# Per-layer embedding of a two-layer streaming encoder: projection before the gates, gates folded into h one by one

## What is computed

```python
for i in range(DEPTH):                       # DEPTH = 2
    h = h + 0.5 * swiglu(rms_norm(h, norm_ff1[i]), w1_ff1[i], w3_ff1[i], w2_ff1[i])
    z = rms_norm(h, norm_mix[i]) @ w_in[i]
    mix = concat([fox_attention(..), s5_mixer(..), retention(..), swa_sink_attention(..)])   # from z
    h = h + mix @ w_out[i]
    h = h + 0.5 * swiglu(rms_norm(h, norm_ff2[i]), w1_ff2[i], w3_ff2[i], w2_ff2[i])
    # per-layer embedding: p is (DEPTH, BATCH, 512, 256), w_ple_proj 256x1024, w_ple_gate 1024x1024
    h = h + (p[i] @ w_ple_proj[i]) * sigmoid(rms_norm(h, norm_ple[i]) @ w_ple_gate[i])
```

## Time and profile before

| | |
|---|---|
| runs (us) | 2390.26, 2395.86, 2398.57; median 2395.86 |
| profiled execution, span from first to last instruction | 2392.5 us |
| PE busy | 2273.6 us (95%) |
| PEld, DVE, ACT, POOL busy | 71%, 40%, 32%, 37% |
| mean granted TensorE clock | 0.954 of full speed |
| HBM traffic | 189.09 MB read, 2.10 MB written, 80 GB/s |

### The profile page before, as it was taken

The page is one execution under the profiler, slowest core; times in us unless marked ns, Lnnn a source line. Parts: engine busy times, 40 slices in busy tenths (PEclk is TensorE's granted clock), DMA queues, the critical chain, the costliest instruction groups (busy, mean ns, idle before and its releaser), DMA issues.

```text
span 2392.5 us, 26535 instructions
## 1 busy us (share of the span) xinstructions
PE 2273.6 (95%) x9180; PEld 1692.2 (71%) x9180; DVE 962.3 (40%) x1296; ACT 769.3 (32%) x1080; POOL 891.0 (37%) x388
## 2 busy tenths in 40 slices
PE   7999999878899999999989999997798999999999
PEld 5888887444457888888868888874454578888887
DVE  5222224868355422222362222248673553222124
ACT  4333223211253333322343332232113443333222
POOL 3444444433102444444344444444331034444442
PEclk9999999888789999999999999998897899999999
DMA  4222333111101222233222223331111022222332
GB/s 137 97 96 96 95 91 122 47 35 44 51 1 53 97 96 96 94 97 99 80 80 98 95 97 96 96 117 45 44 36 50 1 72 95 96 96 93 97 95 84
DMA packets 56087, 192.13 MB, mean 80 GB/s; under 512 B 6216, under 2 KB 6344, under 8 KB 55760
## 3 DMA queue, kind: packets, MB, share of 16 engines
q1 hardware_dynamic: 51840, 180.38, 23.4%
q10 hardware_dynamic: 4176, 10.84, 1.4%
HBM read 189.09 MB, written 2.10 MB: 80 GB/s over the span
## 4 chain that ended last, share of the span: by engine, by line
PE 42%; issue 37%; POOL 15%; DVE 4%; ACT 1%; POOLq 1%; DMA 0%; DVEq 0%; ACTq 0%; SPq 0%
PE psum L658 36%; POOL w_lo L591 14%; PE psum L814 2%; PE psum L717 1%; DVE s5b L1342 1%; PE psum L715 1%; POOL s5sin L611 1%; POOL s5cos L611 1%; DVE s5cos L1344 1%; DVE s5a L1340 0%; PE psum L728 0%; PE psum L905 0%; POOLq L590 0%; DVE s5sin L1345 0%; PE psum L744 0%
## 5 line engine op out<-in xcount | busy, mean ns | idle before, releaser
L591 POOL TENSOR_TENSOR w_lo<-w_raw,w_hi 128x1024 fp32r<-128x1024 f32 (+2 forms) x352 | 831.6, 2364 | 1469.2 <-ACT w_hi L954 1469.1
L658 PE MATMUL psum<-xh,w_hi 128*128 128x512 f32 x1856 | 734.6, 396 | 25.0 <-DVE xl L1178 25.0
L658 PE MATMUL psum<-xl,w_hi 128*128 128x512 f32 x1856 | 725.5, 391 | 0.0
L658 PE MATMUL psum<-xh,w_lo 128*128 128x512 f32 x1856 | 725.4, 391 | 0.0
L954 ACT ACTIVATE w_hi<-w_raw 128x1024 fp32r<-128x1024 f32 (+2 forms) x352 | 359.9, 1022 | 729.1 <-PE psum L658 706.2
L658 PEld LDWEIGHTS psum<-xh,w_hi 128*128 128x128 f32 x1856 | 350.0, 189 | 126.8 <-DVE xl L1178 28.9
L658 PEld LDWEIGHTS psum<-xl,w_hi 128*128 128x128 f32 x1856 | 350.3, 189 | 74.7 <-issue 2.9
L658 PEld LDWEIGHTS psum<-xh,w_lo 128*128 128x128 f32 x1856 | 350.1, 189 | 73.6
L658 PE MATMUL psum<-gh,w_lo 128*128 128x512 f32 x704 | 278.1, 395 | 0.0
L658 PE MATMUL psum<-gh,w_hi 128*128 128x512 f32 x704 | 278.1, 395 | 0.0
L658 PE MATMUL psum<-gl,w_hi 128*128 128x512 f32 x704 | 278.1, 395 | 0.0
(11 more groups left out here) (218 smaller groups left out, 1842.5 us busy)
## 6 DMA issues: line engine op xcount, KB each, us to landing
w_raw<-in_w SPq DMA_DIRECT2D x208, 512.0 KB, 3.3
w_raw<-in_w SPq DMA_DIRECT2D x64, 448.0 KB, 3.3
w_raw<-in_w_in SPq DMA_DIRECT2D x40, 512.0 KB, 3.3
w_raw<-in_w_out SPq DMA_DIRECT2D x16, 512.0 KB, 3.3
w_raw<-in_w_gate SPq DMA_DIRECT2D x16, 512.0 KB, 3.2
h<-in_x_t ACTq DMA_DIRECT2D x8, 256.0 KB, 8.0
dec<-in_decay ACTq DMA_DIRECT2D x2, 1024.0 KB, 5.2
w_raw<-in_w_proj SPq DMA_DIRECT2D x8, 256.0 KB, 2.6
```

The lines of the kernel that those rows point to most:

```text
L591: nc.gpsimd.tensor_tensor(lo[:, 0:tiles, :], raw[:, 0:tiles, :], hi[:, 0:tiles, :].bitcast(F32), ALU.subtract).then_inc(*w_ready.inc(times))
L658: mm = nc.tensor.matmul(out_ap, w[:, t, :], x[:, k0 + t, :], start=(first and t == picks[0] and n == 0), stop=(last and t == picks[-1] and ...
```

## The change

The projection units come first in the per-layer embedding, ahead of the gate units, in the loads, the splits and on PE. ACT copies the projection tiles out of PSUM into SBUF (`proj`, in the feed-forward's buffer, which is free by then); they rotate over banks 0, 1 and 2. `ph` and `pl`, the two parts of p, move to the small work area and are made right behind the last gate tile of the feed-forward's first half. Then the norm's matmul and the gate units follow. DVE takes each gate through to `h` at once: times `rstd`, wait for ACT's sigmoid (in place, in `t_sig`), times `proj`, added to `h`. PE signals in the last gate unit after each tile that this tile of `xh`/`xl` has been read (`x_free`), and ACT waits for this before it writes `xh` of the next layer. The number of matmuls, activations for gates, weight bytes and units is as before; 8 activations (copies) per layer are new.

```diff
@@ tables and banks
+U_PROJ = 4
-    return 4 if u >= BASE["ple"] + KD else 8
+    return 4 if BASE["ple"] <= u < BASE["ple"] + U_PROJ else 8
     b.claim(("norm", "ple"), 3)
     for dt in range(KD):
+        b.claim(("proj", dt), dt % 3, closes=(dt % 2 == 0))
         b.claim(("gate", dt), 4 + dt % 2, closes=False)
-        b.claim(("proj", dt), 6 + dt % 2, closes=(dt % 2 == 0))
+        ph = place("ph", [P, 2, T], m_off, F32R)
+        pl = place("pl", [P, 2, T], m_off + 2 * ROW, F32R)
+        t_sig = place("t_sig", [P, 2, T], m_off + 8 * ROW)
-        ph = place("ph", [P, 2, T], g_off, F32R)
-        pl = place("pl", [P, 2, T], g_off + 2 * ROW, F32R)
-        gate = place("gate", [P, KD, T], g_off + 4 * ROW)
+        proj = place("proj", [P, KD, T], g_off)
...
@@ PE
+                    if free and t != picks[-1]:
+                        mm.then_inc(*free.inc())
...
                 ff(L, 1)
-                for dt in range(KD):
-                    ps = open_bank(L, ("gate", dt))
-                    unit(L, BASE["ple"] + dt, dt, ps[:], xh, xl, 0, KD, True, True, x_done(L, 3) if dt == 0 else None)
-                    if dt == 0:
-                        norm(L, "ple", 3)
                 pe.wait_ge(*p_ready.at(L, 1))
-                for q in range(4):
-                    pe.wait_ge(*w_ready.at(L, BASE["ple"] + KD + q + 1))
+                for q in range(U_PROJ):
+                    pe.wait_ge(*w_ready.at(L, BASE["ple"] + q + 1))
...
+                norm(L, "ple", 3)
+                for dt in range(KD):
+                    ps = open_bank(L, ("gate", dt))
+                    unit(L, BASE["ple"] + U_PROJ + dt, dt, ps[:], xh, xl, 0, KD, True, True,
+                         x_done(L, 3) if dt == 0 else None, free=x_free if dt == KD - 1 else None)
@@ ACT
                 act.wait_ge(*h_ready.at(L, KD * (n - 1) + k + 1))
+                if n == 0 and k < KD - 1:
+                    act.wait_ge(*x_free.at(L, k + 2 - KD))
+                elif n == 0:
+                    act.wait_ge(*unit_done.at(L, 0))
                 nc.scalar.activation(xh[:, k, :], h[:, k, :], ACT.Copy, scale=gain[:, k:k + 1])\
...
                 feed_forward(L, 1)
+                act.wait_ge(*silu_ready.at(L, 2 * NF))
+                act.wait_ge(*p_in.at(L, 1))
+                nc.scalar.activation(ph[:], p_raw[:], ACT.Copy).then_inc(*ph_ready.inc())
                 for k in range(KD):
                     for u in range(3):
                         high(L, BASE["ffb1"] + 3 * k + u + SLOTS)
                     prepare(L, 3, k, par[:, PAR["g_ple"]])
-                act.wait_ge(*p_in.at(L, 1))
-                act.wait_ge(*unit_done.at(L, BASE["ple"]))
-                nc.scalar.activation(ph[:], p_raw[:], ACT.Copy).then_inc(*ph_ready.inc())
+                for k in range(KD):
+                    if k % 2:
+                        act.wait_ge(*unit_done.at(L, BASE["ple"] + k // 2 + 1))
+                        ps = psum[banks.bank[("proj", k)]]
+                    else:
+                        ps = full(L, ("proj", k))
+                    nc.scalar.activation(proj[:, k, :], ps[:], ACT.Copy).then_inc(*proj_ready.inc())
+                    if k % 2:
+                        high(L, BASE["ple"] + k // 2 + SLOTS)
                 root(L, "ple")
                 for k in range(KD):
                     act.wait_ge(*tg_ready.at(L, k + 1))
-                    nc.scalar.activation(gate[:, k, :], t_gate[:, k % 2, :], ACT.Sigmoid).then_inc(*sg_ready.inc())
-                    high(L, BASE["ple"] + k + SLOTS)
+                    nc.scalar.activation(t_sig[:, k % 2, :], t_sig[:, k % 2, :], ACT.Sigmoid).then_inc(*sg_ready.inc())
+                    if k < KD - SLOTS:
+                        high(L, BASE["ple"] + U_PROJ + k + SLOTS)
@@ DVE
-                add_and_prepare(L, 2, "ffb1", par[:, PAR["g_ple"]], 3, 0.5)
+                dve.wait_ge(*gl_ready.at(L, 2 * NF))
                 dve.wait_ge(*ph_ready.at(L, 1))
                 V.tensor_tensor(pl[:], p_raw[:], ph[:].bitcast(F32), ALU.subtract).then_inc(*p_ready.inc())
+                add_and_prepare(L, 2, "ffb1", par[:, PAR["g_ple"]], 3, 0.5)
                 invert(L, 4)
                 for k in range(KD):
-                    dve.wait_ge(*unit_done.at(L, BASE["ple"] + k + 1))
-                    if k >= 2:
-                        dve.wait_ge(*sg_ready.at(L, k - 1))
-                    V.tensor_tensor(t_gate[:, k % 2, :], psum[4 + k % 2][:], rstd[:], ALU.mult)\
-                        .then_inc(*tg_ready.inc())
-                for k in range(KD):
+                    dve.wait_ge(*unit_done.at(L, BASE["ple"] + U_PROJ + k + 1))
+                    t = t_sig[:, k % 2, :]
+                    V.tensor_tensor(t, psum[4 + k % 2][:], rstd[:], ALU.mult).then_inc(*tg_ready.inc())
                     dve.wait_ge(*sg_ready.at(L, k + 1))
...
-                    V.tensor_tensor(t_up[:, k % 2, :], ps[:], gate[:, k, :], ALU.mult).then_inc(*pm_ready.inc())
+                    dve.wait_ge(*proj_ready.at(L, k + 1))
+                    V.tensor_tensor(t, t, proj[:, k, :], ALU.mult).then_inc(*pm_ready.inc())
                     dve.wait_ge(*pm_ready.at(L, k + 1))
-                    V.tensor_tensor(h[:, k, :], h[:, k, :], t_up[:, k % 2, :], ALU.add).then_inc(*h_ready.inc())
+                    V.tensor_tensor(h[:, k, :], h[:, k, :], t, ALU.add).then_inc(*h_ready.inc())
```

More of the change, by code:

```diff
@@ L499, in trunk_kernel @@
         sg_ready = signal("sg_ready", KD)
+        proj_ready = signal("proj_ready", KD)
+        x_free = signal("x_free", KD - 1, before=KD - 1)
         dve_step = signal("dve_step", DVE_STEPS)
@@ L527, in trunk_kernel @@
             reader[("gate", i)] = (tg_ready, i + 1)
[L528 removed]
+            reader[("proj", i)] = (proj_ready, i + 1)
         for f in range(2):
@@ L635, in _ @@
             pe.sem_inc(unit_done.sem, SLOTS)
+            pe.sem_inc(x_free.sem, KD - 1)
             def open_bank(L, key):
```

15 lines of the change are left out of this document (4 added, 11 removed).

## The result

The changed kernel took 2401.53 us (median of 8 runs, 2394.96 to 2404.71); the kernel before, on the same chip beside it, 2391.15 us (8 runs, 2385.78 to 2398.57). The ratio is 1.0037, with a 95% interval of 1.0021 to 1.0053: slower by some 9 us. The forecast was 2398.4 us with a range to 2403.5, so the time lies in the range, but the forecast difference was +2.5 us, and the measured one is three and a half times that. That the time lies in the range is partly luck: the forecast stood on a median of 2395.86 us from three runs, 4.7 us above that of the eight, and with 2391.15 us in its place the range would have ended at 2398.8 us. Slower by over 0.3% had been given 0.14.

What follows compares the result with a forecast made beforehand. The prediction took PE, busy for 95% of the span, as the bound. Program's end +0.9, border +0.3 and clock +1.3 made +2.5 us on 2395.86, so 2398.4 us, range 2391 to 2403.5.

Steps and rivals of the forecast that it cites:

- part 4: Behind the layer border: PE idles 2 us longer and runs longer at half clock, +1.3 us, bounds 0 and +2.8.
- Part 1: Per-layer embedding: waits for banks go, nothing stops PE, its last matmul starts 1.87 and 0.54 us earlier.
- S: Start of PE's last matmul of a layer, 1202.40 and 2387.85 before; forecast 1200.53 and 2387.31.
- rival C: Gate stage: late loads delay root and `rstd`, PE waits before the third gate; 2404.4 us, chance 0.05.
- Part 2: Last gate's way to `h` after PE's last matmul: longer, adding +0.9 us at the program's end.
- Part 3: Border between layers: the next layer's first split and `par` come later, last `xl` at S + 20.25, +0.3 us.
- rival B: Border: copy of `par` locked out behind POOL's `w_lo` of unit 0; +5.7 us, 2401.6 us, chance 0.28.
- rival A: Border and end: the longer tail is hidden and PE's earlier finish counts in full; -3.8 us, 2392.1 us, chance 0.17.
- The sum: Whole program: end +0.9, border +0.3 and clock +1.3 make +2.5 us, giving 2398.4 us.

Runs made afterwards that it cites:

- experiment 2: Kernel before with a memset and a reciprocal on DVE ahead of the copy of `par` at each layer's start: 2394.12 us, ratio 1.0022.
- experiment 4: Extra matmuls: 4 ahead of the projection in the kernel before, 2392.62 us (1.0000); 11 behind the norm in the changed kernel, 2408.23 us (1.0061).
- experiment 6: DVE memsets ahead of a retention product: changed kernel, first product, two 1.0030, one 1.0029; second product, two 1.0035; kernel before, first product, two 0.9999.

## Why the prediction was right or wrong

Layer 1's mixers, matmul 1357 to 2600, in us, over all profiles:

| the source of | profiles | layer 0 | layer 1 |
|---|---|---|---|
| the kernel before (itself twice, late start, 4 matmuls, pause at the first product) | 5 | 412.3, 413.8, 406.6, 411.6, 414.0 | 404.8, 405.2, 405.3, 404.9, 404.9 |
| the changed kernel (itself twice, splits ahead, 11 matmuls, no `x_free`, two with a pause at the first product) | 7 | 410.7, 409.0, 414.1, 414.0, 413.9, 410.0, 414.3 | 408.7, 409.0, 414.5, 413.7, 413.9, 410.9, 413.8 |

The pause at the second product (409.7 and 409.0 us) is left out of the table. Means of layer 0: 411.7 and 412.3, little difference in this scatter. Means of layer 1: 405.0 and 412.1, 7.0 us apart. Some 4.6 us of this are what the tail is longer behind equal clocks; the rest comes with the 17.1 us stretch at matmul 1926, which layer 1 of the changed kernel has in five profiles of seven and layer 1 of the kernel before in none. In layer 0 the kernel before has it more often, four times of five against four of seven, and this hides the difference there.

With the +1.5 us of the change's own terms and the clock behind the border, +1.1 us on average (see part 4 below), the 7.0 us make +9.6, against +9 and +11 measured in the first two comparisons (1.0037 and 1.0045). Closer than a microsecond or two this agreement can't be: each profile is of one run, and three of the changed kernel's lie 6.6 us below and 6.7 and 6.1 us above the medians of their runs.

- *Part 1, PE done earlier:* right. S comes 1.89 and 0.55 us sooner; 1.87 and 0.54 were forecast. The splits of gates 2 and 3 did wait for their loads, 1.44 and 0.58 us, the root ran at 15.6 us after the stage's start (16 forecast), and PE waited for none of it; rival C did not occur. In rows of ACT after:

```profile
1150.99 1.06 ACT L966 ACTIVATE w_hi<-w_raw 128x1024 fp32r<-128x1024 f32 x1 [1.44 <-DMA w_raw<-in_w_gate]
1153.60 1.06 ACT L966 ACTIVATE w_hi<-w_raw 128x1024 fp32r<-128x1024 f32 x1 [0.58 <-DMA w_raw<-in_w_gate]
...
1155.97 0.60 ACT L972 ACTIVATE rstd<-psum 128x512 f32<-128x512 f32 x1
```

- *Part 2, the tail behind S:* right, S + 3.23 against S + 3.31 forecast; +0.83 us of the end's sum against +0.9.
- *Part 3, the border:* right in its chain, 0.45 us short in its length, S + 20.70 against S + 20.25. The branch back on ACT took 2.39 us, where I had counted 1.78, and the first split came at S + 5.5 in place of S + 4.9. The copy of `par` came first and wasn't held up, so rival B did not occur. Nor did rival A: its signs were `par` before S + 5 or the last `xl` before S + 19.
- *`x_free`:* right, nothing.
- *Part 4, the clock behind the border:* right in kind and near in size, though the first profile alone says otherwise (from the last `xl` to `t_gate` 11.81 us, as before). Over the seven profiles of the changed kernel whose border is unedited this stretch took 11.8 to 14.7 us, 12.9 on average; in all five of the kernel before it took 11.8. That is +1.1 us, where +1.3 with bounds of 0 and +2.8 was forecast.
- *The sum:* this step failed. It took the clock as a matter of the stretch behind the border alone, and put the mixers at nothing without a reason: their source is unchanged, but their clock differs from layer to layer. The mixers of layer 1, 300 us further on, took 7.0 us more on average. The view that would have shown the risk, the same stretch in both layers of the one profile before (412.3 against 404.8 us for the same instructions), was there to be read. The direction came true by terms that hold about a quarter of the difference.

What is shown: most of the excess sits in the mixers of layer 1, and in lengths of low clock. What is not settled is why the source of the kernel before has the good case in layer 1 of each of its five profiles. A start of the layer 4 us later did not take it away (experiment 2), and one 2.5 us later did not give it to the changed kernel (experiment 4). Behind equal clocks the tails go with the two sources, which differ by 0.09 us at matmuls 2334 and 2426, and moving the first of these points gave the tails back and lost most of it ahead of them (experiment 6). A build of the changed kernel with the registers placed as before would part the two; it wasn't tried.

The Trainium skill (TensorE: Matmul & The Clock Gate, "What's actually happening") says that the penalty of the clock's ramp is under 1% of a typical kernel's span, and that a model should not be fitted to one count of slow matmuls. What the runs show is of that order, though it is a difference between two kernels and not the whole penalty: 7.0 of 2391 us are 0.3%. For a change whose own terms are 1.5 us it was the larger part.

## What to carry to other kernels

When an edit shortens one wait by a microsecond or two in a kernel that is 95% bound by TensorE, compare the layers of one profile first: stretches of equal work with unequal times (here 57.2, 61.8 and 64.7 us) are the resolution with which such an edit can be forecast, and a shift may bring another of the lengths. Take more than one profile of each kernel, too: the slow clock behind the border, which the first profile after did not have, was in four of the seven. An edit that adds signals can also change the instructions of code that it does not touch. And before work is taken out ahead of a loop's end, look at what stands behind it: hiding the head of the next iteration gave 11.5 us here, the waits for banks 2.4.

## What the hardware showed that I had not expected

- The mixers' tail takes one of three lengths for the same 200 matmuls: 57.1 to 57.4, 61.7 to 61.9 and 64.7 us, with a mean granted clock of 0.88, 0.81 and 0.76. The last is this row of the kernel without `x_free`:

```profile
1877.23:1941.94 64.71, 60.71 (x203) 33.78 (x201) 28.04 (x77) 25.19 (x67) 0.00 (x0) 0.76 0.00 1
```

- Between the falls the time is exact: 286.91 us for matmul 100 to 1357 and 400.9 to 401.1 us for 2600 to 4347, in both layers of all these profiles.
- Where a register instruction stands between a semaphore and the instruction that waits for it, that instruction starts 0.08 to 0.09 us later on DVE (4.84 against 4.76 us behind matmul 2318), and PE's next matmul is later by as much (5.59 against 5.50 us).
- The branch back of a loop took ACT 2.39 us from the end of the last sigmoid to the table load, and DVE 2.48 us to the copy of `par`.
